# Weight units of one size, three buffers, and gate chunks by feature block in a PE-bound decoder layer

## What is computed

```
pr  = split_projection(x @ w_in)            # 1024 -> q, k, v, z and g of all branches
y   = o * silu(pr['z'])                     # o: the five branches' attention outputs
u   = einsum('btnc,ncd->btnd', y, w_branch) # 256 -> 1024 for each branch
out = sum_n(sigmoid(pr['g']) * u) @ w_out
x   = layer_norm(DN_ALPHA * x + out)
```

## Time and profile before

| | us |
|---|---|
| median of three runs | 1481.57 |
| the profiled execution | 1478.38 |
| its span | 1476.6 |
| TensorE busy | 1428.6 (97%) |
| VectorE busy | 645.9 (44%) |
| ScalarE busy | 597.0 (40%) |
| GpSimd busy | 477.8 (32%) |

### The profile page before, as it was taken

The page is one execution under the profiler, slowest core; times in us unless marked ns, Lnnn a source line. Parts: engine busy times, 40 slices in busy tenths (PEclk is TensorE's granted clock), DMA queues, the critical chain, the costliest instruction groups (busy, mean ns, idle before and its releaser), DMA issues.

```text
span 1476.6 us, 18049 instructions
## 1 busy us (share of the span) xinstructions
PE 1428.6 (97%) x6880; PEld 1120.9 (76%) x6880; DVE 645.9 (44%) x1577; ACT 597.0 (40%) x1244; POOL 477.8 (32%) x211
## 2 busy tenths in 40 slices
PE   6999999999999999999999999999999999999995
PEld 5876877777877678877888678777787767788884
DVE  5566644332226433334376664542322534333355
ACT  3454434334345354433145443443333443544222
POOL 3322342223322233333353134323223232332433
PEclk8999999999999999999999999999999999999998
DMA  5311220222212213222322112211212221131411
GB/s 218 115 58 58 86 96 20 72 80 75 67 49 72 72 47 114 72 88 98 119 60 83 58 57 86 86 58 51 100 52 66 64 80 61 46 104 38 157 58 57
DMA packets 67125, 114.31 MB, mean 77 GB/s; under 512 B 2784, under 2 KB 26720, under 8 KB 67040
## 3 DMA queue, kind: packets, MB, share of 16 engines
q1 hardware_dynamic: 67040, 113.16, 23.1%
HBM read 111.05 MB, written 2.10 MB: 77 GB/s over the span
## 4 chain that ended last, share of the span: by engine, by line
PE 90%; DVE 5%; DMA 2%; ACT 1%; issue 1%; POOL 1%; SPq 0%; ACTq 0%; DVEq 0%
PE product L600 21%; PE product L602 19%; PE product L601 19%; PE scores L800 9%; PE context L828 5%; PE transposed L813 3%; PE branch_product L600 2%; PE branch_product L601 2%; PE branch_product L602 2%; PE transposed L743 1%; DMA values_and_gates<-in_ln_b_dram 1%; DVE index_scores L1155 1%; DVE norm_stats L1078 1%; PE scores L762 1%; DVE residual L1084 1%
## 5 line engine op out<-in xcount | busy, mean ns | idle before, releaser
L578 POOL TENSOR_TENSOR weights_rest<-raw_weights,weights_head 128x1024 fp32r<-128x1024 f32 (+3 forms) x176 | 407.6, 2322 | 933.2 <-ACT weights_head L851 933.2
L600 PE MATMUL product<-weights_head,stationary_head 128*128 128x512 f32 (+3 forms) x768 | 302.1, 393 | 0.1
L602 PE MATMUL product<-weights_head,stationary_rest 128*128 128x512 f32 (+3 forms) x768 | 285.9, 372 | 0.0
L601 PE MATMUL product<-weights_rest,stationary_head 128*128 128x512 f32 (+3 forms) x768 | 285.9, 372 | 0.0
L600 PE MATMUL product<-stationary_head,weights_head 128*128 128x512 f32 x640 | 278.6, 435 | 0.0
L602 PE MATMUL product<-stationary_head,weights_rest 128*128 128x512 f32 x640 | 251.0, 392 | 0.0
L601 PE MATMUL product<-stationary_rest,weights_head 128*128 128x512 f32 x640 | 250.5, 391 | 0.0
L851 ACT ACTIVATE weights_head<-raw_weights 128x1024 fp32r<-128x1024 f32 (+3 forms) x176 | 176.2, 1009 | 98.0 <-PE product L602 74.5
L968 ACT ACTIVATE probabilities<-probabilities,negated_maxima 128x256 f32<-128x256 f32 (+3 forms) x160 | 88.4, 552 | 254.5 <-DVE negated_maxima L1189 254.2
L600 PEld LDWEIGHTS product<-weights_head,stationary_head 128*128 128x128 f32 x768 | 145.2, 189 | 39.8 <-issue 18.8
L602 PEld LDWEIGHTS product<-weights_head,stationary_rest 128*128 128x128 f32 x768 | 145.1, 189 | 24.2
(11 more groups left out here) (158 smaller groups left out, 1700.0 us busy)
## 6 DMA issues: line engine op xcount, KB each, us to landing
raw_weights<-in_w_in_dram SPq DMA_DIRECT2D x52, 1024.0 KB, 5.2
raw_weights<-in_w_in_dram SPq DMA_DIRECT2D x36, 512.0 KB, 4.0
raw_weights<-in_w_branch_dram SPq DMA_DIRECT2D x20, 512.0 KB, 3.6
raw_weights<-in_w_out_dram SPq DMA_DIRECT2D x8, 1024.0 KB, 5.8
merged<-in_w_mem_kv_dram SPq DMA_DIRECT2D x4, 1024.0 KB, 9.8
raw_weights<-in_w_in_dram SPq DMA_DIRECT2D x4, 832.0 KB, 4.7
raw_weights<-in_w_in_dram SPq DMA_DIRECT2D x4, 592.0 KB, 9.6
residual<-in_x_dram SPq DMA_DIRECT2D x4, 512.0 KB, 11.2
```

The costliest lines, as they stand in the source:

```text
L578: nc.gpsimd.tensor_tensor(WL[:, sw, half], RAW[:, sr, half], WH[:, sw, half].bitcast(F32), ALU.subtract).then_inc(lo_done.sem, lo_done.ste ...
L600: nc.tensor.matmul(dst, sh, mh, start=start, stop=False)
L601: nc.tensor.matmul(dst, sh, ml, start=False, stop=False)
L602: return nc.tensor.matmul(dst, sl, mh, start=False, stop=stop)
```

## The change

A unit of weights is now a chunk's 256 input rows (2 x 512 elements) and, in a gate chunk, one block of 128 features: all eight k steps of `w_in` and the two of `w_branch`, 10 x 128 = 1280 elements. RAW, WH and WL have three slots of 1280. A chunk has four units `u`. In a plain chunk a unit has four groups, one per tile, of six matmuls; the tiles all end in the last unit. In IX the first two units, and in O1 the last two, alternate tile by tile. In a gate chunk a unit has five groups: four of two k steps into G0 or G1 in turn, and a fifth with the branch product into U. `split` is one piece per unit, placed behind the last group of the unit three before it, and waits until that unit has been used. The separate branch weights, their load and `splitb` are gone. The transposes of the outputs of B, C and D go to banks G2 and G3. PLACES is written anew in the new numbers; the copies of the merged branches to XTH and XTL (`mj`, O's input) stand in the last unit of gD1, two to a group, as their blocks come free.

```diff
 PLACES = [
-    ("index scores", ("E", 0, 2, 0), ("A0", 0, 2, 1), 0.0),
-    ("E attention", ("A1", 0, 0, 0), ("A0", 1, 2, 1), 0.0),
-    ("A queries and keys", ("A0", 1, 3, 1), ("B1", 0, 1, 0), 0.0),
-    ("B queries and keys", ("B0", 1, 2, 1), ("gE0", 0, 1, 0), 0.0),
-    ("D heads", ("gA1", 1, 0, 0), ("gA1", 1, 3, 1), 0.0),
-    ("D norms", ("D0", 1, 1, 0), ("D1", 0, 2, 1), 0.0),
-    ("D attention", ("gC0", 0, 2, 0), ("gD0", 0, 1, 1), -0.1),
-    ("D out", ("gD0", 0, 0, 1), ("gD0", 1, 0, 0), 0.0),
+    ("index scores", ("E", 1, 0), ("A0", 1, 1), 0.0),
+    ("E attention", ("A1", 0, 0), ("A0", 3, 1), 0.0),
+    ("A queries and keys", ("A0", 3, 3), ("B1", 0, 2), 0.0),
+    ("B queries and keys", ("B0", 3, 1), ("gE0", 0, 2), 0.0),
+    ("D heads", ("gA1", 2, 0), ("gA1", 3, 3), 0.0),
+    ("D norms", ("D0", 3, 1), ("D1", 0, 2), 0.0),
+    ("D attention", ("gC0", 0, 1), ("gC1", 3, 2), 0.0),
+    ("D out", ("gC1", 3, 4), ("gD0", 0, 2), 0.0),
...
+def size(c):
+
+    return 10 * P if c[0] == "g" else 2 * WIDTH[c]
...
-        extra[at[(c, kh, 0, 0)]].append(("split",) + halves[i] + (0,))
-        extra[at[(c, kh, 1, 0)]].append(("split",) + halves[i] + (1,))
-        if c[0] == "g" and kh == 0:
-            extra[at[(c, 0, 1, 0)]].append(("splitb", c))
+    for old, new in zip(WEIGHTS, WEIGHTS[3:]):
+        extra[at[old + (parts(old[0]) - 1,)]].append(("split",) + new)
+
+    start = [("split",) + w for w in WEIGHTS[:3]]
...
-NRAW, NW = 2, 2
+NRAW, NW = 3, 3
+UNIT = 10 * P
...
+        def y_bank(b, t):
+
+            return (f"G{2 + t % 2}", G[2 + t % 2]) if b in "BCD" else ("TP", TP)
...
+                    elif item[0][0] == "g":
+                        c, u = item
+                        col = int(c[2]) * 512 + u * P
+                        view = RAW[:, s, :].rearrange("p (k n) -> p k n", k=10)
+                        sp.dma_start(view[:, 0:8, :], w_in[L, :, CHUNKS[c][0][0] + u * P:CHUNKS[c][0][0] + (u + 1) * P].rearrange(
+                            "(k p) n -> p k n", p=P)).then_inc(sem.sem, sem.step(("half", c, u), 16))
+                        sp.dma_start(view[:, 8:10, :], w_branch[L, BRANCH[c[1]], :, col:col + P].rearrange(
+                            "(k p) n -> p k n", p=P)).then_inc(sem.sem, sem.step(item, 16))
...
+                        if c[0] == "g":
+                            wh, wl = (buf[:, sw, :].rearrange("p (k n) -> p k n", k=10) for buf in (WH, WL))
+                            if t < 4:
+                                if t == 0:
+                                    claim(f"G{u % 2}")
+                                for k in range(2 * t, 2 * t + 2):
+                                    last = product3(G[u % 2][:], wh[:, k, :], wl[:, k, :], XTH[:, k, :], XTL[:, k, :],
+                                                    k == 0, k == KD - 1)
...
+                            else:
+                                claim("U")
+                                if u == 0:
+                                    pe.wait_ge(rest.sem, rest.at(L, ("y", c[1], NT - 1)))
...
                     if kind == "split":
-                        item, piece = step[1:3], step[3]
+                        item = step[1:]
                         rw = raw[raw_slot(item)]
                         act.wait_ge(rw.sem, rw.at(L, item))
...
+                        unread(act, L, item)
+                        n = size(item[0])
+                        copy(WH[:, w_slot(L, item), 0:n], RAW[:, raw_slot(item), 0:n]).then_inc(head.sem, head.step(step))
```

More of the change, by code:

```diff
@@ L121, with parts @@
 PLACES = [
[25 rows of a table removed]
-]
-def plan():
-    groups = [(c, kh, t, part) for c in ORDER for kh in range(2) for t in range(NT) for part in range(2)]
[25 rows of a table added]
+]
+WEIGHTS = [(c, u) for c in ORDER for u in range(4)]
+def parts(c):
+    return 5 if c[0] == "g" else 4
+def size(c):
+    return 10 * P if c[0] == "g" else 2 * WIDTH[c]
+def plan():
+    groups = []
+    for c in ORDER:
+        pairs = {"IX": (0,), "O1": (2,)}.get(c, ())
+        for u in range(4):
+            if u in pairs:
+                groups += [(c, u + i, t) for t in range(NT) for i in range(2)]
+            elif u - 1 not in pairs:
+                groups += [(c, u, t) for t in range(parts(c))]
     at = {g: i for i, g in enumerate(groups)}
@@ L210 @@
 PLAN = plan()
-SPLITS = [(c, kh) for c in ORDER for kh in range(2)]
 def loads():
@@ L219, in loads @@
             out.append(("prm", 0))
-        out.append((c, 0))
-        out.append((c, 1))
-        if c[0] == "g":
-            out.append(("wb", c))
+        out += [(c, u) for u in range(4)]
         if c == "gA1":
@@ L639, in _ @@
-                        if part == 0:
-                            continue
-                        last.then_inc(gemm.sem, gemm.step((c, kh, t)))
-                        if kh == 1:
+                        if c == "O0" and t == 0:
+                            pe.wait_ge(rest.sem, rest.at(L, ("m", 2 * u + 1)))
+                        wh, wl = (buf[:, sw, 0:2 * w].rearrange("p (k n) -> p k n", k=2) for buf in (WH, WL))
+                        n = slice(t * P, (t + 1) * P)
+                        for k in range(2):
+                            kk = 2 * u + k
+                            last = product3(G[t][:, 0:w], XTH[:, kk, n], XTL[:, kk, n], wh[:, k, :], wl[:, k, :],
+                                            kk == 0, kk == KD - 1)
@@ L643, in _ @@
+                        last.then_inc(gemm.sem, gemm.step((c, u, t)))
+                        if u == 3:
                             if c in ("A0", "B0", "C0", "IX"):
                                 freed[f"G{t}"] = (copied, L, (c, t))
-                            elif c[0] == "g":
-                                freed[f"G{t}"] = (act_out, L, (c, t))
                             elif c[0] == "O":
@@ L652, in _ @@
                                 freed[f"G{t}"] = (used, L, (c, t))
-                            if c[0] == "g":
-                                claim("U")
-                                if t == 0:
-                                    pe.wait_ge(lo_done.sem, lo_done.at(L, ("wb", c)))
-                                    pe.wait_ge(rest.sem, rest.at(L, ("y", c[1], NT - 1)))
-                                for k in range(2):
-                                    last = product3(U[:], WBH[:, k, n], WBL[:, k, n], YTH[:, k, :], YTL[:, k, :],
-                                                    k == 0, k == 1)
-                                last.then_inc(u_done.sem, u_done.step((c, t)))
-                                freed["U"] = (used, L, (c, t))
                     elif kind == "mkv":
@@ L703, in _ @@
                         _, b, t = step
-                        claim("TP")
+                        name, bank = y_bank(b, t)
+                        claim(name)
                         pe.wait_ge(final.sem, final.at(L, (b, t)))
                         for i in range(2):
-                            last = nc.tensor.transpose(TP[:, i * P:(i + 1) * P], VZ[:, vz(b), t, BW + i * P:BW + (i + 1) * P], ident)
+                            last = nc.tensor.transpose(bank[:, i * P:(i + 1) * P], VZ[:, vz(b), t, BW + i * P:BW + (i + 1) * P], ident)
                         last.then_inc(t_done.sem, t_done.step(step))
-                        freed["TP"] = (rest, L, ("y", b, t))
+                        freed[name] = (rest, L, ("y", b, t))
                     elif kind == "ixj":
@@ L1260, in _ @@
                     elif kind == "grp":
-                        _, c, kh, t, part = step
-                        if kh == 0 or part == 0:
+                        _, c, u, t = step
+                        if u < 3 and c[0] != "g":
                             continue
```

179 lines of the change are left out of this document (76 added, 103 removed), and 34 rows, old and new, of the table PLACES.

## The result

The changed kernel takes 1525.48 us (median of four runs, 1523.29 to 1529.11), the kernel before 1481.84 in the same session: ratio 1.0295, 95% interval 1.0272 to 1.0318. It is 3% slower. The forecast was 1486.4 us with a range of 1471 to 1498, so the prediction was wrong by 39 us; even its slower rival, 1494.4, is 31 us short.

What follows compares the result with a forecast made beforehand. TensorE was taken as the bound, busy 1428.6 of 1476.6 us, its matmuls without a gap. Gains and losses summed to +4.8 us on 1478.4, 1483.2 profiled and 1486.4 for the median; range 1471 to 1498.

Steps and rivals of the forecast that it cites:

- (a): Bank U in gate chunks: more product matmuls between branch products, so TensorE's waits for it go; gain 3.5 us.
- (b): Branch output transposes of B, C and D leave bank TP for G2/G3, so TP's two waits go; gain 1.9 us.
- (e): End of B0: rotation held by GpSimd's split delays the first query-key transpose; 2.3 us a layer, 4.7 in all.
- (g): End of IX: tile 0 ends later, its index transposes stay; wait 2.6 us, not 1.9; 1.5 us in all.
- (f): End of D0: VectorE's queue of value and rotation work delays score steps and D1; 1.7 us a layer, 3.5 in all.
- (d): Returns to product matmuls after transpose or score steps: more of them, counted as 24 x 0.1 = 2.4 us lost.
- Small rows: Rival: gate loads in 512-byte rows take over 16.7 us and TensorE waits; +88 us at 20 us, chance 0.03.
- the split's cover: Gate units: each split is done two gate units (14 us) before TensorE needs it, so it costs nothing.
- (c): Index stage (E/A1/A0): moved splits cut score waits for the maximum from 5.2 to 1.8 us; gain 3.4 us.
- (h): Evacuation bursts in E and A1, and closer spacing of the `du`/`dj` steps; 1.5 us lost, bounds 0 and 5.
- bursts in full: Slower rival: VectorE held at the end of every chunk that rotates, A0's tail included; 1494.4 us, chance 0.27.
- at nothing: Items priced at zero: same total elements copied and subtracted, split cover, kernel start, and hidden gate loads.

Runs made afterwards that it cites:

- e1: The changed kernel with GpSimd's weight rests filled with zeros instead of subtracted: 1467.43 us.
- e2: The kernel before with GpSimd's rests of weights and branch weights filled with zeros instead of subtracted: 1457.17 us.
- e3: The changed kernel with gate loads taken as rows of 2 KB and 1 KB, same bytes and number of DMAs: 1523.38 us.
- e8: e1 with idle VectorE additions meant to lengthen two TensorE waits per layer, one addition in layer 0 and two in layer 1: 1472.05 us.
- e6: The changed kernel with each GpSimd subtraction cut into five pieces, 256 columns for a gate unit: 1486.99 us.
- e4: The changed kernel with the step making branch B's queries and keys begun two groups later: 1519.94 us.

## Why the prediction was wrong

**Most of the waits that it named came.** Bank U's (a) and TP's (b) are gone. B0's end (e): forecast 2.3 us a layer, measured 2.53, by the mechanism described, a 64-column product held until GpSimd was done. IX (g): 2.6 forecast, 2.9 measured. D0 (f): 1.7 forecast, 1.80 measured, and this agreement is luck. The sum of (f) had no instruction held by GpSimd, only VectorE's queue. In the trace the last instruction of the rotation (L1068, 32 columns) takes 1.14 us in place of 0.19 beside a subtraction; without subtractions (e1) the wait is 0.85 us. Half of the forecast was there, the other half came from the cause that (f) had left out. For the returns (d) the prediction's own count gives 191 before and 215 after in each layer (203 less 12, 221 less 6), so 48 more in two layers, not 24; the traces have 394 and 442, 48 more. At 0.09 us that is 4.3 us, not 2.4. The 3.6 us beside waits and clock, and the 1.7 between e1 and e2, are in its neighbourhood and no more than that. Small rows, the split's cover and the loads cost nothing, as said: e3 is within 2 us, and no wait for a weight or a load is new.

**Step (c) was low.** It left 0.9 us a layer in the index stage; measured are 1.4 for the maxima at 109 us, behind a held index sum as described, and 1.1 and 0.3 for the ReLU at 83 and 89. That is 3.9 us more in two layers. Of the ReLU's 2.9 us 1.9 are there without the subtractions too (e1); they stand where (h) put 1.5 us.

**First failed step: the search stopped at the ends of chunks.** (e) to (g) looked at the ends of B0, D0 and IX, where a chunk's tiles are rotated. But a subtraction meets whatever VectorE does beside it, and the attention of A and C has two-input instructions in chains as well. Put at nothing by the forecast, in layer 0: 0.76 us at 165 (A0's rotation, which the rival "bursts in full" did name, at 2.4), 1.72 at 340, 0.81 at 440, 1.41 at 482, 2.60 at 496, 0.59 at 520 and 1.75 at 555, in all 9.6 us, and 9.9 in layer 1. Ahead of each stands an instruction held by a subtraction. With the waits of (a) to (g) as forecast (+0.9), the 3.9 of (c) and 1.1 at the start that is 25.4 us, against 25.0 measured; smaller differences on both sides cancel. "Bursts in full" had the right sign, but its price was taken from rotations too, and halved. The walk that was made for the returns, over the whole list, should have been made for every split, with the question what VectorE has in its queue for the 3 us beside it.

**Second failed step: no price for the clock.** Each wait was counted at its own length. The clock added about 1.7 us to most of the long ones (1.7 to 2.9 us), and its part grew by 19 us in all, nearly as much as the waits. The rows for it were in the trace of before: its waits of 1.9 us at the end of IX are followed by a stretch at half clock (the two of the same length in the index stage are not). The view by 40 slices hides it, since a slice of 38 us with 3.4 us at half still shows 9. "TensorE's busy time within 3 us of before" was the sign set for this, and it failed at 22.6 us.

**Third: length was held to be neutral.** The text said under "at nothing" that elements copied and subtracted are the same in sum. So they are, and it doesn't matter: the same sum in pieces of 256, 512, 1024 and 2048 columns gives 1465.7, 1470.2, 1481.8 and 1531.3 us in the order of before (the last with its place changed too). In the order of the change the step from 1024 to 1280 columns is worth 8.8 us of the 43.6. The larger part, some 25 us, is where the new order puts the subtractions; the last 10 are there also without them (e1 against e2: 5.4 us of idle time, 3.0 of clock, 1.7 of the rest; all of the clock's part there is in the first 40 us). These three shares come from single edits and are added up; no run shows that they add.

Left open: which feature of the order makes the time fall when all splits begin later, and what decides whether a given wait brings the clock down. The clock's part is from one profiled run of each kernel, and the same wait had a stretch in one layer or run and none in another, so a difference of one or two stretches (1.7 us each) between two kernels shows nothing.

## What to carry to other kernels

Where a long GpSimd instruction that reads SBUF runs beside a TensorE-bound kernel, its busy share says nothing; ask for each single one which two-input VectorE instructions can meet it and who waits behind them, and keep it short: cutting it cost 98 us more of GpSimd's time in the kernel before and gained 16 us of the kernel's. Price a new TensorE wait at its length plus what the trace at hand shows behind waits of that length at the lower clock (here 1.7 us behind 9 of 12 waits of 1.7 us and more, and behind 2 of 4 in the kernel before), and look for that in windows of one or two microseconds. An edit that gives larger units or other places to background work should be timed at several places of that work before its size is judged: here the place alone, three groups later, moved the time by 33 us.

## What the runs showed of the hardware

- A VectorE instruction with two SBUF inputs that meets a GpSimd subtraction ends with it, whatever its own size: 2.84 us for one column (0.22 free), 2.41 for 64 (0.22 free), 3.07 for 256 (0.43 free). The instructions of L1315, one input of which is in PSUM, take 687 ns in the changed kernel and 688 in e1: not held.
- With GpSimd's subtractions following each other in pieces, VectorE gets in between two of them, one instruction at a time (0.61 to 0.74 us for each that takes 0.2 alone).
- A GpSimd fill of 1280 columns takes 1.17 us, a subtraction 2.94; pieces of 256 take 0.76, so that five take 3.8.
- Behind the start every stretch at half clock stands at a TensorE wait or shortly behind one, in all eighteen traces; 63 of 94 waits of 1.65 us and more had one. Most lasted some 3.4 us. Two waits of 0.8 us, 2.4 us apart, had one (e8), one of 0.85 alone had none (e1), and one of 0.93 alone had one (e6). One stretch lasted 10 us behind a wait of 1.7 us; the same wait had one of the usual length in e4, and in layer 1 of the changed kernel none.
